# Output projection of a two-layer hybrid backbone: first weight tile ahead of the mixture, first two output tiles side by side with the contraction block outside

## What is computed

```python
mix_x = jnp.concatenate([o_ret, merge_heads(o_mla), merge_heads(o_gqa)], axis=-1) @ w_out[i]
if not last:
    ...
    mix_c = jnp.concatenate([o_ret_c, merge_heads(o_mla_c), merge_heads(o_gqa_c)], axis=-1) @ w_out[i]
    ctx = ctx + mc[2] * mix_c
    ...
x = x + mx[2] * mix_x
```

## Time and profile before

| | before |
|---|---|
| median of 3 runs | 3946.09 us (3945.66 to 3949.57) |
| span of the profiled execution | 3941.5 us |
| PE busy | 3540.9 us (90% of the span) |
| DVE busy | 2487.8 us (63%) |
| ACT busy | 1250.1 us (32%) |
| POOL busy | 669.9 us (17%) |

### The profile page before, as it was taken

The page is one execution under the profiler, slowest core; times in us unless marked ns, Lnnn a source line. Parts: engine busy times, 40 slices in busy tenths (PEclk is TensorE's granted clock), DMA queues, the critical chain, the costliest instruction groups (busy, mean ns, idle before and its releaser), DMA issues. The chain is left out here.

```text
span 3941.5 us, 49189 instructions
## 1 busy us (share of the span) xinstructions
PE 3540.9 (90%) x18524; PEld 2974.4 (75%) x18524; DVE 2487.8 (63%) x3355; ACT 1250.1 (32%) x2126; POOL 669.9 (17%) x284
## 2 busy tenths in 40 slices
PE   2899977999698999999998899869997799999996
PEld 2687776888576888888887577769996577777774
DVE  5655544677427999998866523437784366666666
ACT  1432133667313112111121432316673222222222
POOL 0111120000111222232221111210001132222331
PEclk9899988999899999999999899979998899999998
DMA  5235335121201122112110323424112111111111
GB/s 189 93 120 194 146 78 169 41 50 38 102 19 59 64 77 82 64 65 90 43 33 16 119 94 135 153 66 140 47 36 91 33 48 38 42 48 48 48 48 43
DMA packets 97226, 306.58 MB, mean 78 GB/s; under 512 B 11840, under 2 KB 40384, under 8 KB 95296
## 3 DMA queue, kind: packets, MB, share of 16 engines
q1 hardware_dynamic: 97088, 304.69, 23.6%
HBM read 240.29 MB, written 64.36 MB: 77 GB/s over the span
## 5 line engine op out<-in xcount | busy, mean ns | idle before, releaser
L117 POOL TENSOR_TENSOR wlo<-raw,whi 128x1024 fp32r<-128x1024 f32 x190 | 490.0, 2596 | 1787.1 <-ACT whi L106 1787.0
L145 PE MATMUL up_acc<-h_hi,whi 128*128 128x512 f32 (+1 forms) x1760 | 654.7, 372 | 37.6 <-POOL wlo L117 18.6
L1672 DVE SCALAR_TENSOR_TENSOR xT<-down_acc,mod,xT 128x512 f32<-128x512 f32 (+1 forms) x880 | 562.2, 696 | 177.6 <-PE down_acc L147 174.7
L146 PE MATMUL up_acc<-h_lo,whi 128*128 128x512 f32 (+1 forms) x1760 | 649.9, 369 | 0.0
L147 PE MATMUL up_acc<-h_hi,wlo 128*128 128x512 f32 (+1 forms) x1760 | 649.3, 369 | 0.0
L106 ACT ACTIVATE whi<-raw 128x1024 fp32r<-128x1024 f32 x190 | 200.0, 1056 | 763.6 <-PE down_acc L147 351.0
L145 PEld LDWEIGHTS up_acc<-h_hi,whi 128*128 128x128 f32 x1760 | 333.1, 189 | 103.6 <-ACT up L1599 45.3
L147 PEld LDWEIGHTS up_acc<-h_hi,wlo 128*128 128x128 f32 x1760 | 332.8, 189 | 56.3
L146 PEld LDWEIGHTS up_acc<-h_lo,whi 128*128 128x128 f32 x1760 | 333.2, 189 | 54.2 <-issue 0.2
L145 PE MATMUL proj_acc<-h_hi,whi 128*128 128x512 f32 (+1 forms) x920 | 343.0, 373 | 28.3 <-DVE h_lo L353 15.5
L145 PE MATMUL down_acc<-hid_hi,whi 128*128 128x512 f32 (+1 forms) x880 | 333.1, 379 | 19.9 <-POOL hid_lo L1525 19.9
(11 more groups left out here) (191 smaller groups left out, 5916.4 us busy)
## 6 DMA issues: line engine op xcount, KB each, us to landing
raw<-in_w_mlp SPq DMA_DIRECT2D x132, 512.0 KB, 3.9
norm_buf<-in_w_ada SPq DMA_DIRECT2D x52, 768.0 KB, 4.7
raw<-in_w_proj SPq DMA_DIRECT2D x42, 512.0 KB, 5.7
proj_scratch<-stage SPq DMA_DIRECT2D x18, 640.0 KB, 3.6
xT<-in_xT SPq DMA_DIRECT2D x2, 5120.0 KB, 27.0
ada_raw<-in_w_ada SPq DMA_DIRECT2D x12, 768.0 KB, 4.5
raw<-in_w_mix SPq DMA_DIRECT2D x16, 512.0 KB, 6.2
xT<-proj_scratch SPq DMA_DIRECT2D x4, 1920.0 KB, 8.6
```

The costliest lines, as they stand in the source:

```text
L117: nc.gpsimd.tensor_tensor(self.lo[k][:, :], self.raw[k][:, :], self.hi[k][:, :].bitcast(f32), ALU.subtract).then_inc(self.lo_ready, 1)
L145: nc.tensor.matmul(out, hi, xhi, start=start, stop=False)
L146: nc.tensor.matmul(out, hi, xlo, start=False, stop=False)
L1672: nc.vector.scalar_tensor_tensor(xs, db[g % DB][:, :w], mod_of(layer, 5, m, c), xs, ALU.mult, ALU.add).then_inc(added, 1)
```

## The change

The order of work at the start of the output projection is altered on three engines; what is computed, the number of matmuls, of transfers and of splits stay the same.

- SP issues weight tile 0 first, then mixture blocks 0 and 1, weight tile 1, blocks 2 and 3, weight tile 2. The remaining transfers are as before.
- ACT makes `whi` of tile 0 before `o_hi` of block 0, `whi` of tile 1 before block 2, `whi` of tile 2 before block 4.
- PE works on output tiles 0 and 1 together: for each block `kb` it waits for `o_lo` of that block and then issues the products of tile 0 (all chunks) and tile 1 (all chunks), each chunk into a bank of its own (six banks; four in the last layer). Tiles 2 to 7 are as before.

```diff
             @block.sync
             def _(sp):
-                for kb in range(4):
+                ring.load(sp, 0, 0, 0)
+                for kb in range(2):
                     sp.dma_start(o_raw[kb][:, c0_:], mix[kb, :, c0_:]).then_inc(o_in[kb], 16)
-                for u in range(RING):
-                    ring.load(sp, 0, 0, u)
+                ring.load(sp, 0, 0, 1)
+                for kb in range(2, 4):
+                    sp.dma_start(o_raw[kb][:, c0_:], mix[kb, :, c0_:]).then_inc(o_in[kb], 16)
+                ring.load(sp, 0, 0, 2)
...
             @block.scalar
             def _(act):
                 for kb in range(KB):
+                    if kb in (0, 2, 4):
+                        ring.split_hi(act, 0, 0, kb // 2)
                     act.wait_ge(o_in[kb % 4], 16 * (kb // 4 + 1))
                     nc.scalar.activation(o_hi[:, kb, c0_:], o_raw[kb % 4][:, c0_:], ACT.Copy).then_inc(o_hi_done, 1)
-                    if kb < RING:
-                        ring.split_hi(act, 0, 0, kb)
...
             @block.tensor
             def _(pe):
-                g = 0
-                for m in range(KB):
+                pair = [ring.ready(pe, 0, 0, 0)]
+                for kb in range(KB):
+                    pe.wait_ge(o_lo_done, kb + 1)
+                    for m in range(2):
+                        if kb == 0 and m:
+                            pair.append(ring.ready(pe, 0, 0, 1))
+                        whi, wlo = pair[m]
+                        for i, (c, c0, w) in enumerate(chunks):
+                            wk = slice(kb * P, (kb + 1) * P)
+                            mm = three_pass(banks[m * nch + i][:, :w], whi[:, wk], wlo[:, wk],
+                                            o_hi[:, kb, c0:c0 + w], o_lo[:, kb, c0:c0 + w], kb == 0, kb == KB - 1)
+                            if kb == KB - 1:
+                                mm.then_inc(group_done, 1)
+                g = 2 * nch
+                for m in range(2, KB):
                     whi, wlo = ring.ready(pe, 0, 0, m)
                     for c, c0, w in chunks:
                         if g >= 6:
                             pe.wait_ge(added, g - 5)
                         for kb in range(KB):
-                            if m == 0 and c == chunks[0][0]:
-                                pe.wait_ge(o_lo_done, kb + 1)
```

## The result

The changed kernel takes 3916.67 us (median of 4 runs, 3915.34 to 3921.65) against 3945.88 us for the kernel before (4 runs, 3945.52 to 3949.57). The ratio is 0.9932, with a 95% interval from 0.9919 to 0.9944.

The account below looks back on a forecast made before the run. PE was taken as the bound, losing time to late operands and half clock at the output projection's start. Gains of 14.4 us (first layer) and 8.3 us (last) took 3946.1 to 3923.4 us, range 3917.5 to 3932.5.

Parts of the forecast that it names:

- The bound and the places: Output projection: PE bounds; it loses time waiting for first operands and at half clock; its gain is the kernel's gain.
- Arrival of the operands: First layer: transfers arrive in issue order, weight tile 0 after 3.58 us; PE starts at about 1030.7, not 1035.8.
- the signs named: First layer, if right: PE's long wait about 12.3 us, ending before 1031, half-microsecond wait before tile 1, third tile near 1063.
- The clock: Pair of tiles: PE stays at 1.2 GHz for 4.4 us from tile 1's start, then runs at 2.4 GHz.
- the other reading: Lower end for the pair's half-clock time: 4.4 us from the very first matmul, making the gain 3.7 us larger.
- The price of bank changes: Pair: 0.019 us a change, from the MLP's down tile; 0.9 us in the first layer, 0.6 us in the last.
- The sum: Both output projections: 14.4 us gained in the first layer, 8.3 us in the last, together 22.7 us.
- The end of the range: Low end 3917.5 us: gain of 27.9 us gives 3918.2, less 0.4 us for the spread of the runs.
- The rule against the change: Trainium skill's advice to do one output tile's contraction tiles together; by it the pair stays at or near half clock.
- The first (transfers share the engines): Rival, chance 0.06: transfers share instead of queueing, all seven land with the last; time 3937.5 us.
- the third (half clock throughout): Rival, chance 0.04: the pair runs at 1.2 GHz throughout, 4.8 and 7.0 us later; time 3957.9 us.
- The second (a part of the effect only): Rival, chance 0.06: clock falls back in the pair or POOL and DVE delay each other; gain 7.7 us, 3938.4 us.

Follow-up runs that it names:

- run 2: Kernel before with only the changed order of transfers and of ACT's splits, PE's loop as before: 3935.8 us, ratio 0.9982.
- run 3: Kernel before with only PE's changed loop over the pair of tiles, transfers and splits in the old order: 3921.7 us, ratio 0.9948.
- run 8: Changed kernel with a bank change at every matmul of the pair from block 1 on, block 0 as in the changed kernel: 3915.1 us, ratio 0.9932.
- run 4: Changed kernel with only the first output tile, not two, done with the contraction block outside: 3916.6 us, ratio 0.9930.
- run 11: Kernel before with seven extra matmuls, results overwritten, ahead in each output projection: 3939.8 us in a single execution.
- run 5: Changed kernel with seven extra matmuls, results overwritten, while PE waits for its operands in each output projection: 3911.5 us, ratio 0.9925.
- run 7: Changed kernel with the three passes outside tiles and chunks, so the bank changes after every matmul of the pair: 3919.9 us, ratio 0.9942.

## Why the prediction was right, and where it was off

**The bound and the places.** Right. The gain sits in the two stages, in PE's first operand (run 2) and its work while the blocks arrive (run 3). The rest of the span changed by 1.1 us, and it spreads by 9.8 us among programs that are the same there.

**Arrival of the operands.** Right within 0.7 us. Transfers came in the order of issue; with my figures weight tile 0 should reach ACT 3.6 us after SP's first issue, it took 1026.77 - 1022.49 = 4.3 us in the first layer and 4.0 us in the last. `wlo` 0 took 2.35 us as reckoned, the turn-taking of DVE and POOL put `o_lo` 0 where it was expected, and tile 1 began after 12.8 and 11.9 us (12.4 and 11.9 forecast). This cost about 0.45 us. Of the signs named, PE's long wait was therefore 13.0 us instead of about 12.3 and ended at 1031.74 instead of before 1031, the half microsecond before tile 1 shows as idle time in the last layer only (0.38 us), and the clock was 1.00 from 1040 to 1062, as named.

**The clock.** The largest of the mis-sized terms. The step was "I take 4.4 us from the start of tile 1". Measured, PE was at full clock 2.3 us after that in the first layer and 1.3 us in the last, which is 5.7 and 4.5 us after the very first matmul, and 3.8 and 5.8 us in the changed kernel's second profile. All four are earlier than the 8 us or so after the first matmul that the step amounts to; they lie around the 4.4 us that I had as the other reading, with a spread of 2 us that no run explains. At half price this gives (4.4 - 2.3) / 2 + (4.4 - 1.3) / 2 = 2.6 us.

**The price of bank changes.** The step "0.019 us each" was wrong: 1.5 us were charged. A unit takes 1.74 us against 1.72 in the first layer, some 0.25 us in all, and 1.36 us as before in the last. Three times as many changes left the stages as long as they were (run 8). What makes the MLP's down tile 0.30 us slower is therefore hardly the change of bank; what it is was not tried.

**The sum.** 22.7 + 2.6 + 1.25 - 0.45 = 26.1 us, against 25.8 us of the two stages. The gain of 29.2 us by the first medians holds 3.4 us more than the stages. The repetition gives 24.7 us by the medians and 26.4 us by the stages, so I take these 3.4 us for the spread of the runs. A step of mine hid it: I took the 4.6 us between the median and the profiled span of before for time that lies around every span. In the changed kernel's profiled run that time is 3916.41 - 3914.6 = 1.8 us; the remaining 2.8 us were the distance of that execution from the median, if the time around the span is the same in both. Without these 3.4 us the median would be 3920.1 us, inside the range instead of 0.8 us below it. The end of the range has a slip of its own: 3918.2 less 0.4 us is 3917.8, not 3917.5.

**The rule against the change.** The Trainium skill's advice in "TensorE: Matmul & The Clock Gate", section "HAM oscillation — how this bites in real kernels", is given for thin products and reads "do all K-tiles for one M-tile before DMA-waiting". I took it for a rule against this change and left that condition out. In the kernel before the waits stand inside the output tile, so its start is not the loop that the page advises. What the page blames, short work between waits, agrees with the traces. With the contraction inside and every operand there the kernel before has full clock:

```profile
1054.20:1160.60 106.40, 106.35 (x548) 91.04 (x546) 14.67 (x23) 5.31 (x5) 12.01 (x5) 1.00 0.03 10
```

I read the prediction's 1.00 "in a long accumulation" from this row, which is missing in the earlier trace rows. With the waits inside the tile the clock is 0.50, and it fell in such a wait even where it was up (run 2, last layer); with the contraction outside it stays at 1.00 (run 4 and the changed kernel). The swinging clock of "A second HAM failure mode: psum-queue depth-cycling", which the page reports for bf16, did not appear with the fp32r operands here, even with a change of bank at every matmul (run 8).

**Rivals.** The first (transfers share the engines) is ruled out by the order of arrival, the third (half clock throughout) by the stretches. The second (a part of the effect only) did not come true in the changed kernel.

## What to carry to other kernels

While the operands of a contraction arrive one block at a time, let the contraction block be the outer loop over as many PSUM banks as give PE more work for a block than a block takes to arrive. Here that was 3.48 us for two output tiles against 2.3 us a block; a single tile, with 1.74 us, already came within about 2 us. Put ahead in the queue what the first matmul needs, but do not expect much of that alone: it brought 7.6 of about 26 us, since PE was still bound by the last block. And before a fraction of a per cent is ascribed to an edit, compare the stage it touches between two meeting points of the engines, because the rest of the same program moved by up to 10 us between executions.

## What the runs showed of the hardware that I had not expected

The granted clock fell inside waits of 5.9 and 3.9 us (run 11, from 1.00 to 0.50 between 1033 and 1034 in the first layer) and inside one of 2.35 us (run 2, last layer), but PE stood at full clock across the waits of 1.24 and 1.55 us in run 5. From the first matmul of the stage to full clock it took 3.8 to 5.8 us in four cases of the same program, and more than 7.1 us where a wait of 2.1 us lay behind the first three matmuls (run 7). And the first transfer of a stage took 4.2 us from issue to use in one execution, 5.3 us in another, with the same queue behind it (the earlier trace rows and run 3), a difference of 1.1 us for everything behind it.
